# Cache gathers started before the memory turns, and the query rotation's half swap done by transfers

## What is computed

```python
cq, ckv, kr, gq, gk, gv, gg, ga, z_mla, z_gla = jnp.split(rmsnorm(x, g_attn) @ w_in, split_idx, axis=-1)
q = (rmsnorm(cq, g_q) @ w_uq).reshape(B, S, 8, 128 + 64)
q_rope = rope(q[..., 128:], pos)                  # halves (x1, x2) -> (x1 cos - x2 sin, x1 sin + x2 cos)
q_lat = jnp.einsum('bshn,rhn->bshr', q[..., :128], w_uk)
c_kv, k_rope = rmsnorm(ckv, g_kv), rope(kr, pos)
# sample tokens: keys are 2048 past rows read from a paged cache by page_table, and their own
keys_lat = concat([cache_lat[page_table], c_kv]); keys_rope = concat([cache_rope[page_table], k_rope])
o_lat = softmax((q_lat @ keys_lat + q_rope @ keys_rope) * scale) @ keys_lat
mem_k, mem_v = rmsnorm(mem, g_mem) @ w_mk, rmsnorm(mem, g_mem) @ w_mv
h = x + (sigmoid(z_mla) * MLA + sigmoid(z_gla) * GLA) @ w_out
h = h + cross_attend(rmsnorm(h), mem_k, mem_v)    # 256 memory rows
h = h + moe(rmsnorm(h))                           # top 4 of 32 experts
```

## Time and profile before

| | |
|---|---|
| time, median of 3 runs | 1360.05 us (1359.65 to 1361.78) |
| the profiled execution | 1358.12 us, span of its instructions 1356.3 us |
| TensorE busy | 1304.1 us, 96% of the span |
| DMA engines busy | 81.1% for SP's queue and 9.7% for POOL's |
| bytes moved | 499 MB, 368 GB/s over the span |

### The profile page before, as it was taken

How to read it: one execution, slowest core, us unless ns; L and a number is a source line. 1 busy time by engine, 2 the same in 40 slices (tenths; PEclk the granted TensorE clock), 3 DMA queues, 4 the chain that set the end, 5 groups by cost and what they waited for, 6 DMA issues and landing times.

```text
span 1356.3 us, 17073 instructions
## 1 busy us (share of the span) xinstructions
PE 1304.1 (96%) x6899; PEld 692.5 (51%) x6899; DVE 364.0 (27%) x796; ACT 253.4 (19%) x566; POOL 101.4 (7%) x133
## 2 busy tenths in 40 slices
PE   9999999999999999999998998989999998998988
PEld 7848887788887344344243433424434343342433
DVE  3864433211456222113021111202212112120212
ACT  4314345221125111011110101101011011010102
POOL 2652221001200000000000000000000000000000
PEclk9999999999999999999999989999999999999999
DMA  9894567548969999999999999999999999999996
GB/s 325 285 363 156 202 242 246 197 145 309 293 234 377 389 417 426 429 428 429 428 429 429 429 428 428 428 429 423 430 428 430 427 430 428 431 427 428 430 425 263
DMA packets 64898, 499.03 MB, mean 368 GB/s; under 512 B 5967, under 2 KB 7352, under 8 KB 39768
## 3 DMA queue, kind: packets, MB, share of 16 engines
q1 hardware_dynamic: 51424, 453.37, 81.1%
q0 software_dynamic: 13216, 44.50, 9.7%
q10 hardware_dynamic: 216, 0.58, 0.1%
HBM read 491.34 MB, written 7.08 MB: 367 GB/s over the span
## 4 chain that ended last, share of the span: by engine, by line
PE 75%; DMA 20%; DVE 1%; POOL 1%; issue 1%; SPq 0%; ACT 0%; ACTq 0%; DVEq 0%; POOLq 0%
PE bank L1348 22%; PE bank L804 17%; PE bank L1368 13%; DMA arena<-in_w_down 10%; DMA ring<-in_w_gate_up 9%; PE bank L1401 4%; PE bank L1332 4%; PE bank L754 1%; PE bank L1357 1%; PE bank L838 1%; PE bank L1363 1%; PE bank L1285 1%; PE bank L1182 1%; PE bank L767 1%; DMA ring<-in_cache_kv_latent,arena 1%
## 5 line engine op out<-in xcount | busy, mean ns | idle before, releaser
L1348 PE MATMUL bank<-ring,arena 128*64 128x512 f32 x1536 | 344.8, 597 | 6.4 <-DMA ring<-in_w_gate_up 6.4
L1368 PE MATMUL bank<-arena 128*64 128x512 f32 x1000 | 229.3, 609 | 30.2 <-DMA arena<-in_w_down 30.2
L804 PE MATMUL bank<-arena,ring 128*128 128x264 f32 x1008 | 230.7, 388 | 0.0
L1348 PEld LDWEIGHTS bank<-ring,arena 128*64 128x64 f32 x1536 | 104.3, 137 | 222.4 <-issue 206.9
L804 PEld LDWEIGHTS bank<-arena,ring 128*128 128x128 f32 x1008 | 189.4, 190 | 36.0 <-issue 4.4
L1368 PEld LDWEIGHTS bank<-arena 128*64 128x64 f32 x1000 | 70.4, 140 | 173.9 <-issue 129.0
L2607 DVE TENSOR_TENSOR resid<-resid,bank 128x264 f32<-128x264 f32 x128 | 54.8, 429 | 355.0 <-PE bank L1401 353.5
L1348 PE MATMUL bank<-arena 128*64 128x512 f32 x512 | 115.5, 593 | 3.5 <-DMA arena<-in_w_gate_up 3.5
L2612 DVE TENSOR_SCALAR arena<-bank 128x512 f32<-128x512 f32 x32 | 22.0, 688 | 340.8 <-PE bank L1348 340.8
L1566 ACT ACTIVATE arena<-bank 128x264 f32<-128x264 f32 (+6 forms) x129 | 51.0, 403 | 165.9 <-PE bank L804 126.8
L1946 ACT COPY arena<-bank 64x512 f32<-64x512 f32 x63 | 36.5, 580 | 232.9 <-PE bank L1368 232.1
(11 more groups left out here) (364 smaller groups left out, 933.2 us busy)
## 6 DMA issues: line engine op xcount, KB each, us to landing
ring<-in_w_gate_up SPq DMA_DIRECT2D x94, 2048.0 KB, 28.9
arena<-in_w_down SPq DMA_DIRECT2D x62, 2048.0 KB, 22.2
arena<-in_w_gate_up SPq DMA_DIRECT2D x32, 2048.0 KB, 28.8
ring<-in_w_in SPq DMA_DIRECT2D x10, 2048.0 KB, 11.4
out<-arena POOLq DMA_DIRECT2D x8, 512.0 KB, 5.0
ring<-v_rows POOLq DMA_DIRECT2D x8, 512.0 KB, 6.0
ring<-in_w_o_mla SPq DMA_DIRECT2D x2, 2048.0 KB, 8.9
ring<-in_w_o_gla SPq DMA_DIRECT2D x2, 2048.0 KB, 15.2
```

The lines of the kernel that those rows point to most:

```text
L804: mm = nc.tensor.matmul(lin_bank(name)[0:m, 0:width], w(ring_name, nk, cols)[:, k, a:a + m], rhs[:, k, 0:width], start=(k == 0), stop=(k = ...
L1348: mm = nc.tensor.matmul(B[i // 2][CAP * (i % 2):CAP * (i % 2) + CAP, :], xg[:, k, CAP * e:CAP * e + CAP], slot(n)[:, a:a + 512], start=Fal ...
L1368: mm = nc.tensor.matmul(bank[CAP * half:CAP * half + CAP, :], hidden[:, k % 4, CAP * (k // 4):CAP * (k // 4) + CAP], weights[:, 512 * half ...
```

## The change

1. **Start.** 5 and 4 zero products in place of 12 and 3. The first row tile of x has a semaphore of its own (`first_x_loaded`); PE turns it for all eight chunks first, and the other two tiles when they are there. ScalarE's queue stays as it was.
2. **Gathers ahead.** The product for `idx` moves between the first and second halves of the input products. Its constants (`spread`, `within`) are loaded by a small transfer of their own ahead of the memory rows, and these land outside the gathers' buffers. POOL starts the gathers as soon as `idx` is there and x has been read. The small weights (7 transfers, before at 8.4 us) are issued behind the fourth gather group, the stores of `c_kv` and `k_rope` behind the sixteenth.
3. **Key turns.** DVE turns key groups earlier: the first right behind `m2`, the second behind `uk0`, and the groups are taken in the order 0, 4, 7, 1, 2, 3, 5, 6.
4. **Rotation.** The four `rot` products and their four copies on ACT are gone. SP issues four transfers within the arena that swap the halves of `q_pairs` into `q_turned`, when `qr3` is copied out; they stand behind `gv0` in SP's queue. The sine table has the sign in it.
5. **Order.** SP loads `mk` ahead of `uq`; PE does `mk2` with `mk1` ahead of `qb`. Two memsets (1536 and 2048 columns) go from DVE to POOL.

```diff
-RING = [("in_a", "kr"), ("uq", "qr3"), ("mk", "mk3"), ("mv", "mv1"), ("gv0", "gv3"), ("gq", "gq3"), ...
+RING = [("in_a", "kr"), ("mk", "mk3"), ("uq", "qr3"), ("mv", "mv1"), ("gv0", "gv3"), ("gq", "gq3"), ...
+KEY_ORDER = (0, 4, 7, 1, 2, 3, 5, 6) + tuple(range(8, 16))
...
+                if name == "gq":
+                    lin_done(sp, "qr3")
+                    for i in range(4):
+                        j = i ^ 1
+                        sp.dma_start(q_turned[32 * i:32 * i + 32, :, :], q_pairs[32 * j:32 * j + 32, :, :]).then_inc(S("q_swapped"), 16)
...
-            pool.wait_ge(S("turn_full"), TI["m7"] + 1)
-            for n in range(16):
-                if n >= 4:
-                    pool.wait_ge(S("keys_turned"), n - 3)
-                gather_past(n, True)
+            pool.wait_ge(S("x_turned"), KC)
+            pool.wait_ge(S("token_sums"), 3)
+            for i, n in enumerate(KEY_ORDER):
+                if i >= 4:
+                    pool.wait_ge(S("keys_turned"), i - 3)
+                gather_past(n, True, i % 4)
+                if i == 3:
+                    load_small_weights()
+                if i == 7:
+                    lin_full(pool, "qr3")
+                    nc.gpsimd.memset(q_blocks, 0.0)
+                    nc.gpsimd.memset(past_wide, 0.0).then_inc(S("q_copies"), 1)
...
-            zero_products(12)
+            zero_products(5)
...
-            zero_products(3)
-            pe.wait_ge(S("x_loaded"), 48)
+            zero_products(4)
+            pe.wait_ge(S("first_x_loaded"), 16)
             for c in range(KC):
                 if c >= 6:
                     turned(pe, f"gains{c - 6}")
-                for tt, (t0, n) in enumerate(TILES):
+                nc.tensor.transpose(X_BANK[c][:, 0:P], x_tok[:, 0, c * P:(c + 1) * P], ident)
+            pe.wait_ge(S("x_loaded"), 32)
+            for c in range(KC):
+                for tt, (t0, n) in list(enumerate(TILES))[1:]:
...
-            for j in range(4):
-                lin_done(pe, f"qr{j}")
-                lin(f"rot{j}", [(con("rot"), q_pairs[:, j, :])], T)
...
-            project(["mk1"], "mk", 8, 512, memT, NMEM, first=P)
+            project(["mk1", "mk2"], "mk", 8, 512, memT, NMEM, first=P)
...
+            turn_keys(4)
+
+            lin_done(dve, "qr3")
+            dve.wait_ge(S("q_swapped"), 64)
             V.tensor_tensor(q_pairs, q_pairs, bc(con("cos")[:, None, :], [P, 4, T]), ALU.mult)
```

More of the change, by code:

```diff
@@ L52 @@
 CONSTS = {}
-for _name, _n in [("ident", 128), ("ones", 128), ("count", 64), ("seat", 1), ("before", 128), ("rot", 128), ("cos", T), ("sin", T),
-                  ("carry", PROMPT), ("causal", 384), ("upto", 64), ("spread", 128),
-                  ("within", 2), ("pick", 8 * 32)]:
+for _name, _n in [("ident", 128), ("ones", 128), ("count", 64), ("seat", 1), ("before", 128), ("spread", 128), ("within", 2),
+                  ("rot", 128), ("cos", T), ("sin", T), ("carry", PROMPT), ("causal", 384), ("upto", 64)]:
     CONSTS[_name] = (sum(n for _, n in CONSTS.values()), _n)
 N_CONST = sum(n for _, n in CONSTS.values())
+N_PAGES = CONSTS["rot"][0]
 KEPT = CONSTS["before"][0] + CONSTS["before"][1]
 A_NORMED, A_TABLE = 19840, 19840 + KC * T
-A_SMALL = A_TABLE + N_CONST - KEPT
+A_SMALL = A_TABLE + N_CONST - KEPT + 256
 MOE_END = 13352
@@ L100, in constants @@
     put("within", (i % 8).astype(f)[:, None] + np.array([0, 0.5], f))
[L101 to L104, removed]
     return c
@@ L118 @@
 LIN = (["cq0", "cq1", "ckv", "kr", "rotk", "mk0"]
-       + [f"qn{h}" for h in range(8)] + [f"qr{j}" for j in range(4)] + [f"rot{j}" for j in range(4)]
-       + [f"ql{h}" for h in range(8)] + ["mk1", "qb", "own0", "own1", "mk2", "mk3", "mv0", "mv1"]
+       + [f"qn{h}" for h in range(8)] + [f"qr{j}" for j in range(4)]
+       + [f"ql{h}" for h in range(8)] + ["mk1", "mk2", "qb", "own0", "own1", "mk3", "mv0", "mv1"]
        + ["ga"] + EARLY[0:2] + [f"la{h}" for h in range(4)]
@@ L142 @@
 TI = {n: i for i, n in enumerate(TURN)}
-RING = [("in_a", "kr"), ("uq", "qr3"), ("mk", "mk3"), ("mv", "mv1"), ("gv0", "gv3"), ("gq", "gq3"), ("gk", "gk3"), ("gv1", "gv7"),
+RING = [("in_a", "kr"), ("mk", "mk3"), ("uq", "qr3"), ("mv", "mv1"), ("gv0", "gv3"), ("gq", "gq3"), ("gk", "gk3"), ("gv1", "gv7"),
         ("uv", "uv7"), ("gg0", "gg3"), ("gg1", "gg7"), ("zm0", "zm3"), ("zm1", "zm7"), ("zg0", "zg3"), ("zg1", "zg7"),
@@ L940, in _ @@
             turned(pe, "krt")
-            project(["mk2", "mk3"], "mk", 8, 512, memT, NMEM, first=2 * P)
+            project(["mk3"], "mk", 8, 512, memT, NMEM, first=3 * P)
             past_scores(0)
@@ L1630, in _ @@
             turn_out("krt", [(kr_tok[:, 0:2, :], P, (0, 128)), (kr_tok[0:8, 2, :], 8, (128, 192))])
-            for j in range(4):
-                out(f"rot{j}", q_turned[:, j, :])
             for h in range(H_MLA):
@@ L1635, in _ @@
             out("mk1", memk[:, 1, :], width=NMEM)
+            out("mk2", memk[:, 2, :], width=NMEM)
             lin_full(act, "qb")
@@ L1651, in past_exp @@
                                      accum_out=past_stat[:, 2 * g + 1:2 * g + 2]).then_inc(S("past_exp"), 1)
-            for h in (2, 3):
-                out(f"mk{h}", memk[:, h, :], width=NMEM)
+            out("mk3", memk[:, 3, :], width=NMEM)
             past_exp(0)
@@ L2100, in memory_turned @@
                     .then_inc(S("turned_by_dve"), 1)
+            dve.wait_ge(S("page_rows"), 1)
+            for i in range(2):
+                V.tensor_scalar(idx[:, :, i, :], SCORE_BANK[:, 0:16].rearrange("p (r b) -> p r b", r=2), con("within")[:, i:i + 1], 2.0, ALU.add, ALU.mult).then_inc(S("idx"), 1)
             inverse_of_rows_at_start(5, [(slice(3, 5), P)])
@@ L2116, in _ @@
             memory_turned(2)
+            turn_keys(0)
             turn_out("uk0", [(ukT[:, 0:512], P, (0, 512))])
-            dve.wait_ge(S("page_rows"), 1)
-            for i in range(2):
-                V.tensor_scalar(idx[:, :, i, :], SCORE_BANK[:, 0:16].rearrange("p (r b) -> p r b", r=2), con("within")[:, i:i + 1], 2.0, ALU.add, ALU.mult).then_inc(S("idx"), 1)
+            turn_keys(1)
             memory_turned(4)
```

103 lines of the change are left out of this document (50 added, 53 removed).

## The result

The changed kernel takes 1367.72 us (median of 5 runs, 1362.74 to 1371.09), the kernel before 1359.65 in the same series (1358.72 to 1361.78). The ratio is 1.0055, 95% interval [1.0033, 1.0077]: slower by some 7.5 us, between 4.5 and 10.5 (the medians differ by 8.1). I had forecast slower, but by 3, and the time lies above my range.

What follows compares the result with a forecast made beforehand. PE's work without holes bounds the opening, full DMA engines the windows from about 480 us. 3.4 late less 0.3 gives +3.1: 1358.12 + 3.1 + 1.9 = 1363.2 us; range 1356.7 to 1366.2, its own 1360.2 to 1364.2.

Steps and rivals of the forecast that it cites:

- my sum of +3.1: Opening up to `mk3` and `past_scores(0)`: PE 3.4 us late at `mk3`, less 0.3 at `past_scores(1)`.
- `past_scores(1)` -0.3: PE's wait for the keys at `past_scores(1)`: 0.3 us saved, since groups 8 to 11 are there earlier.
- What bounds it: Whole kernel: a PE shift in the opening moves the end one for one; nothing before 480 us is made up.
- Start: Turns of x: first tile turned early, ending at 11.1 and not 12.3, 1.2 us gained; bounds 0 and 2.1.
- Gathers: POOL's first gather starts at 19.6 and not 34.11; the second group's last piece lands at 32.3.
- Key turns between memory turns: DVE's row in the memory turns: PE waits, `qn0` starts at 38.8, 1.4 us later, with the start's gain spent.
- Rotation: Between `qn0` and `mk1`: dropping the four `rot` products gains 1.9 us; PE is ready for `qb` at 61.6.
- When the swap lands: Swap in SP's queue: 17.46 MB at 396 GB/s gives 58.5, taken as 59.5; bounds 56.5 and 60.5.
- What waits for it: Ahead of `qb` and `mk3`: PE waits for DVE's rotation, then the copies; `mk3` at 68.9, 3.4 us late.
- more held: Rival: late loads or slow memsets ahead of `past_scores(1)` or the swap cost 3 us more, 1366.2 us; chance 0.15.
- In time: Rival: swap lands in time, `mk3` at 64.9, a gain of 0.9 with `past_scores(1)`, 1359.2 us; chance 0.22.

Runs made afterwards that it cites:

- The kernel with the needless products: Changed kernel with old start, copies of `qb` ahead of two key turns, and 16 needless products ahead of PE's wait for the rotated queries: 1365.46 us, 1.0044.
- The kernel with late gathers: Changed kernel with gathers and key turns at their old places and the old start, rotation still by transfers in SP's queue: 1365.26 us, 1.0044.
- the pair made to show it: Changed kernel with old start and copies of `qb` ahead of two key turns, without and with 16 needless products ahead of `qb`: 1365.95 and 1365.46 us.

## Why the forecast was right in its sign and wrong in its size

The kernel with the needless products gives the best account, as its clock is full and its times lie close together. Its mark is

```profile
110.45 1.47 PE L996 MATMUL bank<-arena 128*128 128x256 f32 x8
```

+6.3 us in its trace, +5.8 by the medians (1365.46 - 1359.65). Of these 6.3, counted down PE's timeline: x and the old start with the new loads +0.6 (row sums at 24.08, before 23.44); key turns in the memory turns +2.5 (`qn0` at 40.47, before 37.38, less the 0.6); `rot` gone -1.8 (`mk1` at 56.30, before 54.99); wait for the swap, filled with products, +3.6 (`qb` at 66.86, where before and 3.5 of `mk2` make 62.0); `mk3` another +0.1; DVE's last key turns ahead of `past_scores(0)` +1.7; less 0.4 at `past_scores(1)`.

Set against my sum of +3.1, in the same places: the start -1.2 forecast and +0.6 measured; key turns +2.6 and +2.5; rotation -1.9 and -1.8; wait ahead of `qb` +1.6 (61.6 to 63.2) and +3.6; wait for DVE behind it +2.3, forecast ahead of `mk3`, and +1.8, nearly all of it ahead of `past_scores(0)`; `past_scores(1)` -0.3 and -0.4. Two terms were mis-sized, the start by 1.8 us and the wait for the swap by 2.0.

- **What bounds it**: right. The opening's delay reached the first expert loads and the end one for one.
- **Start**: wrong, in sign. I had 1.2 us gained. The tile's turns were done early, but the other rows came at 8.68, and PE had 1.8 us of nothing. I had named a clock that rises later, and called it cheap, since a delay would be lost on `mk2`'s end, which waits anyway. The clock did fall, in the kernel before with only this edit too, and the edit alone measured +0.1% and not -0.1%. 1.2 gained against 0.4 (its mark) to 0.9 (its median) lost is a step of some 2 us in the sum. That I read a faster clock from 7 us on rested on the spacing of the products alone; the granted clock of that trace is 1.00 before and behind it. Where I was right is that a late start is lost on a wait: in the changed kernel's trace the row sums come 3.6 us later than with the old start (27.73 and 24.14), and `qb` comes earlier (65.90 and 67.06).
- **Gathers**: first issue at 24.83, not 19.6, from that same clock; with the old start and full clock the index product stands at 20.15, 1.4 us behind my 18.8, and with the second tile of x first the first issue is at 19.11.
- **Key turns between memory turns**: right. DVE's row ran behind as worked out. From the row sums to `qn0` it took 15.4 us in the changed kernel (27.73 to 43.16), 16.4 in the one with products in the hole (24.08 to 40.47) and 13.9 before (23.44 to 37.38): a cost of 1.5 to 2.5, where I had 2.6 (1.4 and the 1.2 it used up). `qn0` came at 43.2, and with the old start at 40.3, not at 38.8: that is the start's share. The Trainium skill (SBUF — State Buffer, section SBUF: two separate sides) says that some DVE operations keep GpSimd from writing a transfer's descriptors; that didn't show: the first eight issues took 0.94 to 1.13 us, no more than the 1.01 to 1.20 of before.
- **Rotation**: 1.9 us gained, right (1.8). PE was ready for `qb` at 63.2 with the old start, forecast 61.6.
- **When the swap lands**: this is the step that failed. I took it as bytes alone, 17.46 MB to be moved at 396 GB/s, and put the landing at 59.5. DVE took the swap up at 60.7 in the changed kernel's trace and at 63.1 and 63.2 in the two with the old start and full clock up to `qb`. The bytes were counted well: by then 17.69 MB had been moved from 12 us on in the first, 18.29 in the one with the old start alone. And what is ahead does count: in the eleven traces with the early gathers and `mk3` behind `qb` the first of the four was issued anywhere from 52.2 to 55.1, and the swap was taken up between 60.7 and 63.3, no earlier for an earlier issue. But it was not all that counts. The kernel with late gathers had moved less by 59.4:

```profile
DMA packets 5931, 15.92 MB, mean 336 GB/s; under 512 B 499, under 2 KB 716, under 8 KB 5928
```

By my rule that is (17.46 - 15.92) / 396 GB/s = 3.9 us ahead of the 58.5 that went with 17.46 MB, so 54.6, and it was 59.4. Two things were missing. The first is the transfer's time from issue to use, 5.7 us in the changed kernel's trace, 9.1 from ScalarE's queue, 9.4 with late gathers, 11.0 with the old start. The second is the rate, which is not 396 GB/s while these transfers move. From 58 to 59 us of the changed kernel's trace nothing but the swap was on the engines, and it kept them 96% taken with 0.20 MB:

```profile
DMA packets 67, 0.20 MB, mean 199 GB/s; under 512 B 20, under 2 KB 20, under 8 KB 67
...
q1 hardware_dynamic: 67, 0.20, 95.7%
```

The row for it wasn't in the trace of before, which has no transfer from one partition group to another. I bounded the landing by bytes on both sides and never by issue plus latency. With the old start PE had 11.0 us of work from the issue to `qb` (52.2 to 63.2), against 11.0 of transfer and 3.8 of rotation, and waited 3.8. How the transfer's time divides into its own and what it shares with `gv0` and the gathers is not shown.
- **What waits for it**: mechanism right, size short. PE idled ahead of `qb` (0 to 3.8 us) and of `mk3` (0 to 2.6). Forecast some 4 in all. Without products in the hole `mk3` started at 69.3 to 72.6 in the kernels with the early gathers and the swap that do it behind `qb`, forecast 68.9.
- **Missing**: `past_scores(0)`. I ended my sum at `mk3`, and with `mk2` taken from behind `qb` the last key turns were no longer hidden: 1.2 to 1.6 us in four kernels in which they stand behind the copies (2.5 with `mk3` ahead of `qb`, none in one whose `mk3` ran at half clock), nothing in the changed kernel, where they stand ahead of them and delay `mk3` instead. It is one cost in two places.
- **The rivals**: "more held", 1366.2, was the nearest, though by another road. "In time" was wrong for this placement, but it is what the kernel with `mk3` ahead of `qb` did, 1360.6 where that rival gave 1359.2. The rule cited for it, from the Trainium skill (DMA: Bandwidth & Descriptors, Rules for kernel authors), holds when one counts how early: 11 us of PE work between issue and wait were too few, 14.3 were enough (50.1 to 64.4, with `mk3` among it). The same page's section "Issuing engines are not separate DMA queues" agrees with the run in which ScalarE's queue brought nothing.

What stays open: the changed kernel measured +8.1, the clean account gives +5.8. By the medians the copies placed first are worth about 1.3 of the difference (1367.27 against 1365.95), which is within the spread of the runs. The remaining 1 us would be the clock's falls, at the start or behind a hole. Each of the traces with the transfers and `mk3` behind `qb` has such a fall somewhere in its opening, at the start, in the memory turns or behind `qb`, but for one with a filled hole, and one of them cost some 4.4 us; but the pair made to show it differed by 0.5 us, so this share is argued, not shown. Nor does the fall need the swap: the traces with products for the rotation and the new start (12 to 15 us) and of the kernel before with the new start have one too. In the kernel with ScalarE's queue the two runs whose granted clock was 0.992 or more on the whole took 1363.0 and 1363.5 us, and the four at 0.986 to 0.989 took 1367.5 to 1371.5. That fits the clock as what spreads these times, but doesn't say what made it fall in the one and not in the other.

## What to carry to other kernels

Before a product on an engine that always has work is replaced by a transfer, ask for the transfer's whole time from its source being ready to its use, and count the work that can stand in between: here 1.9 us of products were traded for a transfer of 6 to 11 us and 11 us of cover, with the rotation's 3.8 us still to come behind it. Count both the bytes ahead of it and its time from issue to landing: here neither alone gave the landing. And follow a moved block both ways: what it now covers, and what it used to cover (`mk2` and the last key turns).

## What the runs showed of the hardware

Four transfers of 132 KB each between partition groups took 2.8 to 9.0 us from each issue to its landing, and 5.7 to 11.0 us from the first issue to the first use. Issue to landing in the kernel with the old start:

```profile
L482 SPq DMA_DIRECT2D arena<-arena x4: 577/592/637, 52.2 to 54.2; - x4
...
DMA to landing us min/median/max: 6.3/6.7/9.0
```

By the Trainium skill (SBUF — State Buffer, section The DMA setup-cost knee) a transfer takes 2 us and its bytes at 436 GB/s, for 132 KB an estimate of 2.3 us; the measured ones are 1.2 to 4 times that, with gathers, weights or both beside them. While the swap went on, the engines were fully taken but moved less than 396 GB/s: 199 when it was alone on them (the rows above), and 227 in this window of the kernel with the old start:

```profile
56.00:60.00 4.00, 4.00 (x20) 3.53 (x19) 0.00 (x0) 0.88 (x3) 1.00 (x2) 1.00 1.06 227
```

In the five traces in which PE idled 1.6 to 3.8 us ahead of `qb`, its clock fell to half within 1.3 us behind the hole and stayed there for 7 to 10 us. Needless products in the hole kept it up. Holes of 2.3 and 2.6 us ahead of `mk3` in two others had no fall behind them, one of 1.4 had, and so had one of 2.5 ahead of `past_scores(0)`. So the length of the hole alone does not tell whether the clock falls.
